# Two paddings in on-chip memory: the weights' pieces and the activations' operands begin at multiples of 512 bytes

## What is computed

```
# first block
h = rms_norm(x, norm_mix);  u = h @ w_in            # 1024 -> 2560: lru_x, lru_g, q, k, v
y_lru = gelu(lru_g) * rg_lru(conv(lru_x))           # recurrence over time
y_att = stick_breaking_attention(q, k, v)           # 8 heads of 64
x = x + concat(rms_norm(y_lru), rms_norm(y_att)) @ w_out
gu = rms_norm(x, norm_ffn) @ w_ffn_in               # 1024 -> 2 x 2816
x = x + (silu(gu[..., :F]) * gu[..., F:]) @ w_ffn_out
x = rms_norm(x, norm_final)
# second block
p = rms_norm(x, g) @ w_in_2                         # conv branch, q, k, v, forget logits, two gates
x = x + (g_conv * y_conv + g_attn * y_attn) @ w_o_2
up = causal_conv(rms_norm(x, g) @ w_up_2)           # 1024 -> 2 x 2816
x = x + (silu(up_a) * up_b) @ w_down_2
out = rms_norm(x, g)
```

## Time and profile before

| | |
|---|---|
| median of three runs | 1256.82 us |
| the profiled execution | 1255.6 us |
| its span, first to last instruction | 1253.8 us |
| PE (TensorE) busy | 1228.0 us, 98%, 7804 matmuls |
| VectorE busy | 991.8 us, 79% |
| ScalarE busy | 670.4 us, 53% |
| moved by DMA | 174.14 MB, 139 GB/s in the mean |

### The profile page before, as it was taken

One profiled execution on the slowest core, in us unless ns is written; L12 is line 12 of the kernel. 1 busy time (PEld: TensorE's weight loads), 2 busy tenths in 40 slices (PEclk: granted clock), 3 DMA queues, 4 the chain that ended last, 5 costly groups with the idle time before them and its releaser, 6 DMA issues.

```text
span 1253.8 us, 19172 instructions
## 1 busy us (share of the span) xinstructions
PE 1228.0 (98%) x7804; PEld 1078.1 (86%) x7804; DVE 991.8 (79%) x1196; ACT 670.4 (53%) x837; POOL 186.0 (15%) x168
## 2 busy tenths in 40 slices
PE   6999999999999999999999999999999999999997
PEld 5778677889999999997899999657888999988886
DVE  6888764888788778887989967566678899989886
ACT  5463674374545445567545535363444666656555
POOL 5003001002222101110122113000000222202020
PEclk9999999999999999999999999999999999999999
DMA  5423201249999779664599857301324799968765
GB/s 172 143 68 98 70 1 34 84 123 194 177 208 184 142 204 248 141 123 118 111 210 197 190 101 206 113 1 34 117 86 151 125 213 194 183 157 173 207 116 137
DMA packets 144458, 174.14 MB, mean 139 GB/s; under 512 B 5370, under 2 KB 118250, under 8 KB 144242
## 3 DMA queue, kind: packets, MB, share of 16 engines
q0 software_dynamic: 58288, 71.33, 35.7%
q1 hardware_dynamic: 86066, 101.58, 24.3%
q10 hardware_dynamic: 16, 0.00, 0.0%
HBM read 170.78 MB, written 2.11 MB: 138 GB/s over the span
## 4 chain that ended last, share of the span: by engine, by line
PE 92%; DVE 4%; ACT 2%; issue 1%; DMA 0%; SPq 0%; ACTq 0%; DVEq 0%
PE psum L2516 12%; PE psum L2522 12%; PE psum L2519 12%; PE psum L2785 11%; PE psum L2783 11%; PE psum L2784 11%; PE psum L2857 3%; PE psum L2859 3%; PE psum L2858 3%; PE psum L3065 2%; PE psum L3066 2%; PE psum L3067 2%; PE psum L2974 1%; PE psum L2660 1%; PE psum L2645 1%; PE psum L2672 1%
## 5 line engine op out<-in xcount | busy, mean ns | idle before, releaser
L990 ACT ACTIVATE w_hi<-raw 128x1024 fp32r<-128x1024 f32 (+2 forms) x121 | 156.2, 1294 | 210.5 <-PE psum L2522 145.6
L1544 DVE TENSOR_TENSOR w_lo<-raw,w_hi 128x1024 fp32r<-128x1024 f32 (+2 forms) x121 | 184.4, 1526 | 57.2 <-ACT w_hi L990 57.2
L2516 PE MATMUL psum<-act_hi,w_hi 128*128 128x512 f32 x520 | 207.7, 399 | 4.3 <-DVE act_lo L1551 1.5
L2522 PE MATMUL psum<-act_hi,w_lo 128*128 128x512 f32 x520 | 204.7, 394 | 0.1
L2519 PE MATMUL psum<-act_lo,w_hi 128*128 128x512 f32 x520 | 203.6, 391 | 0.0
L2785 PE MATMUL psum<-s_hi,w_lo 128*128 128x256 f32 x704 | 194.9, 277 | 0.0
L2783 PE MATMUL psum<-s_hi,w_hi 128*128 128x256 f32 x704 | 194.8, 277 | 0.0
L2784 PE MATMUL psum<-s_lo,w_hi 128*128 128x256 f32 x704 | 194.8, 277 | 0.0
L2785 PE MATMUL psum<-act_hi,w_lo 128*128 128x256 f32 x528 | 146.2, 277 | 0.0
L2783 PE MATMUL psum<-act_hi,w_hi 128*128 128x256 f32 x528 | 146.1, 277 | 0.0
L2784 PE MATMUL psum<-act_lo,w_hi 128*128 128x256 f32 x528 | 146.1, 277 | 0.0
(11 more groups left out here) (411 smaller groups left out, 2672.6 us busy)
## 6 DMA issues: line engine op xcount, KB each, us to landing
raw<-in_w_in SPq DMA_DIRECT2D x15, 1024.0 KB, 5.4
xz<-in_w_ffn_in POOLq DMA_DIRECT2D x24, 512.0 KB, 6.6
raw<-in_w_ffn_in SPq DMA_DIRECT2D x22, 512.0 KB, 5.5
xz<-in_w_up POOLq DMA_DIRECT2D x21, 512.0 KB, 6.1
raw<-in_w_up SPq DMA_DIRECT2D x18, 512.0 KB, 5.2
raw<-in_w_in SPq DMA_DIRECT2D x16, 512.0 KB, 5.0
v<-in_w_in POOLq DMA_DIRECT2D x15, 512.0 KB, 6.2
x_buf<-in_w_ffn_out POOLq DMA_DIRECT2D x6, 1024.0 KB, 9.8
```

Source lines behind the costliest of these rows:

```text
L990: A(w_at(w_hi, s, h, n - h), home(s, n)[:, h:n], ACT.Copy).then_inc(w_hi_ready, 1)
L1544: V.tensor_tensor(w_at(w_lo, s, h, n - h), home(s, n)[:, h:n], w_at(w_hi, s, h, n - h).bitcast(F32), ALU.subtract).then_inc(w_lo_ready, 1)
L2516: ins = mm(dst, stationary[0], moving[0], start=first, stop=False)
L2522: return mm(dst, stationary[1], moving[0], start=False, stop=last)
```

## The change

Two tensors that nothing reads or writes are put into the layout: one of 96 float32 elements (384 bytes in each partition) in front of `w_hi`, one of 112 (448 bytes) in front of `act_base`. `w_hi` and `w_lo` thereby move by 384 bytes, and so do `tmp`, `rstd`, `par` and the constants; `act_hi` and all that is placed from `act_base` on moves by 832. `xT` and `raw` stay. No instruction is added, removed or reordered.

```
         raw = sb("raw", [P, 2, SLAB])
+        sb("w_pad", [P, 96])
         w_hi = sb("w_hi", [P, 2, SLAB], F32R)
         w_lo = sb("w_lo", [P, 2, SLAB], F32R)
...
         gain_both = sb("gain_both", [P, DC])
+        sb("act_pad", [P, 112])
         act_scope = ExitStack()
         act_base = nc.sbuf_base
         act_hi = sb("act_hi", [P, DC, TOKENS], F32R, act_scope)
```

## The result

The change made the kernel slower: 1275.2 us (1274.6 to 1275.31, 4 runs) against 1256.78 (1256.21 to 1257.33, 4 runs), a ratio of 1.0146, interval 1.0128 to 1.0163: 18.4 us lost, where 14.2 were forecast as won.

The account below looks back on a forecast made before the run. PE was busy 98% of the span, so time was the number of matmuls times their spacing. Terms of -7.2, -3.3 and -3.7 us summed to -14.2, giving a median of 1242.6 us; range 1214 to 1277.

Parts of the forecast that it names:

- steps 5 to 7: VectorE and ScalarE indifferent to operand starts, DMA landings hidden, VectorE leaves cover for a faster PE: nothing gained or lost.
- Step 4: The other 3,804 products of 256 columns, near the load's floor: nothing taken, bounds -6.5 and +17.1 us.
- Step 3: Slow stretch of 816 256-column products (618 to 714 us) returns from 117.8 to 113.3 ns: -3.7 us.
- Steps 1 and 2: 512-column matmuls cross fewer multiples of 512: -7.2 us where activations move, -3.3 us where weights move.
- Rival A: Weights' load and moving stream start at the same place and meet in every matmul: slower, 1282 us, chance 0.33.
- step 7: VectorE, busy 91 and 93%, lets PE speed up 1.5 to 2% before being late; the forecast needs 1.1%.

Follow-up runs that it names:

- both_192: Kernel before, with paddings of 64 and 448 bytes: weights and activations both start 192 bytes behind a multiple of 512; 1275.21 us, ratio 1.0155.
- last_only: Kernel before, with a 256-byte gap between the weights' halves and equal operand starts for the last down product alone; ratio 1.0005.
- split_starts: Kernel before, with weights' slabs for 512-column matmuls 64 bytes further on (starts equal to the activations') and a 256-byte gap between halves; ratio 1.0059.

## Why the prediction was wrong

- **The reading of the bound was right.** The time is matmuls times spacing, the clock, VectorE, ScalarE and the DMAs had no part in it (steps 5 to 7), and four spacings account for the loss to 0.4 us.
- **Step 4 failed**, and with it the sign: "The other 3,804 products of 256 columns ... I take nothing". They lost 6.67 ns each (113.3 to 120.0), +25.4 us, beyond the bound of +17.1, because that bound was the worst speed seen at distance +64, and distance 0 has one of its own. That these products sat 1.7 ns above the load's floor was read as "little to win"; with so little above the floor there was much more room to lose than to win. That this chain was in the better of two gaits could be seen from the earlier trace rows.
- **Step 3 failed**: the slow stretch did not return to 113.3 but went to 120.0, +1.8 instead of -3.7 us.
- **Steps 1 and 2 were right in sign, for a wrong reason.** 2.2 ns were won where 3.9 were forecast, and 6.6 where 5.0: -8.4 us against -10.5. Both seats ended at 226.7; the terms had them at about 225 and 228. That these two terms came out near their forecast is luck. But fewer crossings of 512 had nothing to do with it; both_192 crosses as before and wins the same.
- **Rival A named the mechanism's condition**, equal starts, and the right group. One argument for it, "0 lies between them, not beyond the better one", failed: for the 512s, 0 lies beyond the better seat (226.7 against 228.9). Its prices were taken from rows at another distance: 1282 against 1275.2; the 512s gained where it had them lose, the 256s lost more. The evidence that was at hand, and that I weighed too low, was the two speeds of the earlier trace rows: where equal addresses already show two speeds, a move of addresses may cost as easily as win.
- **A slip that cost nothing**: step 7 says that PE may speed up by 1.5 to 2% before VectorE is late; 91 and 93% busy leave 7 to 9%.
- **Why the trace of before could not settle it**: no row in it has distance 0. The sum took a change of alignment as a change of degree; the probe shows a table with neighbours at 113.3 and 120.0.
- **The page that spoke against any effect.** The seats differ, and the cells of the probe range from 113.3 to 120.0 and from 226.7 to 233.3 with nothing but TensorE at work: address and spacing are tied, which the Trainium skill, "TensorE: Matmul & The Clock Gate", section "Step-by-step: what each phase is for", with its two independent read ports, does not lead one to expect. By it the time would have stayed at 1256.8; it rose by 18.4 us. Whether load and stream truly get in each other's way is not shown: stationary slices of 32 columns ran the 256-column blocks at distance 0 in 113.3 in one probe and 117.8 in another, both below 120.0, yet did not help the 512s.

**Open**: what happens inside at each distance; what picks the gait at entry; why distance 112 runs otherwise in the kernel than in the probes. Moving the loads in time against their matmuls was not tried.

## What to carry to other kernels

Where a kernel is bound by the spacing of matmuls, read that spacing exactly, by stage, before and after any change of layout: on-chip addresses alone moved it here by up to 6% (113.3 to 120.0 ns), with the instructions, the clock and the busy share unchanged. Judge such a change by the distance between the starts of the two operands and not by their alignment, and price it for each size apart. Do not bound an unmeasured distance by the measured ones: the slow speed seen before was 4.5 ns above the fast one, and distance 0 cost 6.7. A short program with TensorE alone had the kernel's speeds at distance 0 to the digit and would have told beforehand; at distance 112 it did not, so the kernel itself has the last word. Where one execution shows two speeds for equal work, compare kernels by many runs, since one profile shows one draw.

## What the runs showed of the hardware

- float32r matmuls with a load each, TensorE alone, granted clock 1.00: 113.3 to 120.0 ns for 256 columns and 226.7 to 236.7 for 512, by the operands' starts, once settled.
- The pattern repeats every 256 bytes: +320 equals +64 in the kernel (0.9998), and the table's second half its first but for activations at 320 with weights at 192 or 448.
- Distance 0: 120.0 (256 columns) and 226.7 ns (512) with 128-column loads, in both kernels that lie so throughout and in all probes, whatever ran before; 512-column chains need some ten matmuls to settle there (230.3 to 230.7 over six).
- Distance +64, 256 columns: 113.3 or 117.8 ns by the chain, in the same program too (before, 720 to 776 us); changed by six matmuls at distance 0 (4 of 4) and at both short breaks inside a chain (last_only at 707, split_starts at 668 us).
- A load of 128 columns with a matmul of 128 or 192 columns behind it takes 111.6 to 111.7 ns a pair; with loads of 32 columns the pair took 60.1 (128 columns) and 88.3 (192).
